# First modulation weights loaded ahead, squares summed on TensorE, modulation rows turned one piece later, filter sums by channel

## The chip, the cores and the metric

The kernel runs on one core of a Trainium2 chip. The metric is the device time of one execution in microseconds (us). Work is done by TensorE (PE), VectorE (DVE), ScalarE (ACT) and GpSimd (POOL); SyncE (SP) issues most DMAs. Each engine runs its own instructions in order, and engines wait for each other on semaphores.

## What is computed

Two layers of a generator block over 256 latent and 256 context tokens, width 1024. Cut to what the change touches:

```python
mod = silu(c) @ w_ada[li] + b_ada[li]                 # and the same of c_ctx; 6 pieces of 1024: sh1, sc1, g1, ...
h   = x * rsqrt(mean(x*x) + EPS) * norm1 * (1 + sc1) + sh1
p   = h @ w_in                                        # then four mixers, merge, MLP
# Hyena filters, of both layers and two orders n:
hdn  = sin(freq1 * (sin(freq0 * (feats @ w1 + b1)) @ w2 + b2))
taps = stack of (hdn @ w3) * decay                    # 512 channels
taps = taps / sum(abs(taps), axis=positions)          # one sum for each channel
K    = rfft(taps)
```

## The kernel before

Activations stand as features by tokens: `xT` is 8 pieces k of 128 features by 512 tokens. Weights stream from HBM in strips of 512 KB through the four slots of `raw`. The products of the layers are made of 128x512 matmuls in which both sides are split in a high and a low part (three matmuls for one, line L660, helper `mm3`); other products are plain float32 (L655, helper `mm`), and the trace counts two MATMULs for each of these.

The change lies in the start (`start_` of each engine, ahead of `dn(0)`) and in `dn(0)`, the first product, where filters of the second layer are interleaved by chunk (`between`). In the start PE does, in an order written out by hand: `columns` (turns the small vectors), `filter_angles`, eight pieces `mod_group(0, g)` of the modulation (each two strips of `w_ada`; 8 matmuls of 256 columns, weights 32 columns wide), each followed by `mod_turn(0, g - 1)` of the row before, which ACT has copied in `mod_row`; the turns of x (L766); `filter_taps`, `filter_scale` (the sum of |taps| over all positions, by 4 matmuls with the matrix of ones, after which DVE's `reciprocal` has 128x512 elements), `filter_spectrum` (16 MATMULs in the trace for one order) and `filter_nyquist` (4). The loads of strips wait for the slots of `raw`, which the pieces before must have read; x is loaded after the fourth strip. POOL squares x and adds the squares up (L3397, L3399). When the last piece of the modulation is turned, DVE makes `amp`, POOL multiplies the odd pieces of x with it (L3405) and with `rstd` (L3432), DVE the even ones (L2750), ACT adds the shift and rounds to the high part `hhl`, DVE makes the low part (L2739), and PE's `feature_strips("dn", 0)` follows piece by piece.

Four `work_bank`s of PSUM are filled in order (`fill`); a fill waits until the bank's last reader has given it back.

## Time and profile before

| | us |
|---|---|
| median of 3 runs | 1946.11 (1945.92 to 1949.07) |
| profiled execution, first to last instruction | 1946.3 |
| PE busy | 1873.7 (96%) |
| DVE busy | 1284.9 (66%) |
| ACT busy | 788.5 (41%) |
| POOL busy | 608.5 (31%) |
| 16 DMA engines, mean | 130 GB/s |

A busy PE is one with a matmul in its pipeline; it isn't PE at its full rate. The profile also tells the TensorE clock that was granted, as a share of 2.4 GHz. Before its first record it prints 1.00, whatever the clock was; the durations tell more there.

### The profile page before, as it was taken

What the parts mean: (1) busy time and instruction counts of PE and PEld (TensorE: products, weight loads), DVE (VectorE), ACT (ScalarE), POOL (GpSimd) and SP (SyncE); (2) the same over time, 40 slices, a digit from 0 to 9 for tenths busy, and PEclk for the clock granted to TensorE, in tenths of its full rate; (3) what the DMA queues carried; (4) which work ended last, traced back from release to release, by engine and by line L of the source; (5) the groups of instructions that cost most, each with busy time, mean ns of one, the idle gap of its engine ahead of it and who ended that gap; (6) DMA issues with size and microseconds to landing.
All of it is one profiled execution on the core that took longest, in us unless ns stands there. A gap on an engine that the chain in (4) does not pass through costs nothing.

```text
span 1946.3 us, 32006 instructions
## 1 busy us (share of the span) xinstructions
PE 1873.7 (96%) x11146; PEld 1525.9 (78%) x11146; DVE 1284.9 (66%) x2122; ACT 788.5 (41%) x1627; POOL 608.5 (31%) x553
## 2 busy tenths in 40 slices
PE   6999899999999999999999999999998899999999
PEld 2556788767588888877888887787787789999999
DVE  4754867666856755358765776759686655567574
ACT  2325633356243333333222232356535545445453
POOL 3433243722312111163200223444555521143030
PEclk8999899999999999999999999999999999999999
DMA  6433111232234443344555556233214335554554
GB/s 226 139 107 105 38 56 55 87 121 80 84 130 152 130 161 118 95 134 160 185 173 186 174 194 196 87 87 87 77 44 136 104 109 176 177 168 156 180 183 140
DMA packets 210925, 252.98 MB, mean 130 GB/s; under 512 B 11715, under 2 KB 176900, under 8 KB 209796
## 3 DMA queue, kind: packets, MB, share of 16 engines
q1 hardware_dynamic: 207088, 235.01, 38.2%
q10 hardware_dynamic: 3732, 16.60, 2.3%
q8 instruction: 61, 1.00, 0.2%
q14 instruction: 44, 0.36, 0.1%
HBM read 245.29 MB, written 6.29 MB: 129 GB/s over the span
## 4 chain that ended last, share of the span: by engine, by line
PE 73%; issue 10%; DVE 8%; POOL 5%; ACT 4%; DMA 1%; ACTq 1%; DVEq 0%; POOLq 0%
PE psum L660 58%; PE psum L655 13%; POOL whl L1544 2%; DVE big L2570 2%; PE psum L766 1%; POOL big L3537 1%; ACT whl L1535 1%; ACT big L1783 1%; ACT big L1786 1%; PE psum L628 1%; DVE hhl L2739 1%; DVE big L2579 1%; POOL big L1634 1%; DMA big<-in_hy_table_dram 1%; DVE big L2722 1%
## 5 line engine op out<-in xcount | busy, mean ns | idle before, releaser
L660 PE MATMUL psum<-hhl,whl 128*128 128x512 f32 (+1 forms) x4416 | 826.6, 346 | 11.6 <-DVE hhl L2739 4.3
L660 PEld LDWEIGHTS psum<-hhl,whl 128*128 128x128 f32 x4416 | 693.3, 190 | 132.4 <-issue 24.8
L1535 ACT CAST whl<-raw 128x512 fp32r<-128x512 f32 x656 | 374.1, 618 | 811.6 <-PE psum L660 806.6
L1544 DVE TENSOR_TENSOR whl<-raw,whl 128x512 fp32r<-128x512 f32 x480 | 333.6, 736 | 315.3 <-ACT whl L1535 314.4
L660 PE MATMUL psum<-bigr,whl 128*128 128x512 f32 (+1 forms) x2688 | 474.9, 337 | 1.5 <-DVEq L3314 0.7
L660 PEld LDWEIGHTS psum<-bigr,whl 128*128 128x128 f32 x2688 | 412.8, 190 | 57.2 <-issue 2.2
L1544 POOL TENSOR_TENSOR whl<-raw,whl 128x512 fp32r<-128x512 f32 x176 | 233.6, 1349 | 377.5 <-ACT whl L1535 359.0
L655 PE MATMUL psum<-big 128*128 128x128 f32 (+8 forms) x1572 | 245.7, 326 | 17.9 <-DMA big<-in_hy_w_dram 5.4
L655 PEld LDWEIGHTS psum<-big 128*128 128x128 f32 (+4 forms) x1572 | 164.5, 175 | 77.3 <-issue 51.8
L3537 POOL TENSOR_TENSOR big<-big,tmp 128x512 f32<-128x512 f32 (+1 forms) x64 | 64.5, 1021 | 341.3 <-DVE tmp L3311 340.7
L660 PE MATMUL psum<-whl,hhl 128*128 128x512 f32 x672 | 160.1, 396 | 11.0 <-POOL whl L1544 9.1
L660 PEld LDWEIGHTS psum<-whl,hhl 128*128 128x128 f32 x672 | 125.6, 190 | 40.1 <-POOL whl L1544 12.2
L1786 ACT COPY big<-psum 128x512 f32<-128x512 f32 (+3 forms) x182 | 90.3, 497 | 131.3 <-PE psum L655 93.3
L1596 POOL TENSOR_TENSOR tmp<-tmp 128x512 f32<-128x512 f32 (+1 forms) x32 | 31.3, 979 | 320.1 <-ACT tmp L1783 320.1
L2722 DVE SCALAR_TENSOR_TENSOR big<-big,csil 128x512 f32<-128x512 f32 x112 | 87.9, 785 | 5.2
L1783 ACT ACTIVATE big<-psum 128x512 f32<-128x512 f32 (+3 forms) x142 | 65.9, 475 | 26.3 <-PE psum L655 10.8
L3405 POOL TENSOR_SCALAR big<-xT,amp 128x256 f32<-128x256 f32 x48 | 54.3, 1143 | 37.9 <-issue 26.7
L2703 DVE SCALAR_TENSOR_TENSOR big<-big,csil 128x512 f32<-128x512 f32 x84 | 64.4, 819 | 1.8 <-DVE tmp L3311 1.8
L2570 DVE TENSOR_TENSOR big<-psum,big 128x512 f32<-128x512 f32 (+2 forms) x74 | 47.5, 642 | 22.1 <-PE psum L655 19.1
L2574 DVE TENSOR_SCALAR big<-psum,cols 128x512 f32<-128x512 f32 (+1 forms) x48 | 31.8, 662 | 45.1 <-PE psum L660 27.0
L2579 DVE SCALAR_TENSOR_TENSOR big<-psum,cols,big 128x510 f32<-128x510 f32 (+1 forms) x96 | 58.4, 608 | 2.6
L1783 ACT ACTIVATE big<-psum,small 128x512 f32<-128x512 f32 (+2 forms) x72 | 40.8, 594 | 39.8 <-DVE small L2576 21.7
(187 smaller groups left out, 1524.9 us busy)
## 6 DMA issues: line engine op xcount, KB each, us to landing
raw<-in_w_mlp_dram SPq DMA_DIRECT2D x128, 512.0 KB, 3.8
raw<-in_w_in_dram SPq DMA_DIRECT2D x88, 512.0 KB, 3.7
big<-in_w_ada_dram SPq DMA_DIRECT2D x88, 512.0 KB, 5.1
raw<-in_w_gate_dram SPq DMA_DIRECT2D x64, 512.0 KB, 3.5
raw<-in_w_branch_dram SPq DMA_DIRECT2D x32, 512.0 KB, 3.5
raw<-in_w_ada_dram SPq DMA_DIRECT2D x24, 512.0 KB, 5.3
raw<-in_w_o_dram SPq DMA_DIRECT2D x16, 512.0 KB, 3.5
hy_spectra<-big ACTq DMA_DIRECT2D x2, 2560.0 KB, 9.3
```

What stands on the lines that cost most here:

```text
L655: return nc.tensor.matmul(o_, a, b, start=start, stop=stop)
L660: m = nc.tensor.matmul(o_, a(p_), b(q_), start=first and i == 0, stop=last and i == 2, skip_group_check=shared)
L1535: nc.scalar.copy(whl[:, r, 0, ks], raw_of(n)[:, ks]).then_inc(S["hi_ready"], 1)
L1544: ins = eng.tensor_tensor(whl[:, r, 1, ks], raw_of(n)[:, ks], whl[:, r, 0, ks].bitcast(F32), ALU.subtract)
L1783: return nc.scalar.activation(o_, i_, fn, **kw)
L1786: return nc.scalar.copy(o_, i_)
L2570: step(V.tensor_tensor(o_, a, b, op), s_)
L2579: step(V.scalar_tensor_tensor(o_, a, sc, b, op0, op1), s_)
L2703: V.scalar_tensor_tensor(um_acc[:, r, :] if k == 7 else um_part[:, r, :], um_raw[k // 2][:, k % 2, :], csil[:, k, r:r + 1], um_part[:, r, ...
L2722: ins = V.scalar_tensor_tensor(vm_acc if k == 7 else vm_part, w, c_, vm_part, MUL, ADD)
L3405: ins = G.tensor_scalar(hn[:, k, sl], xT[:, k, sl], amp[:, li, which, k, s_:s_ + 1], None, ALU.mult)
L3537: G.tensor_tensor(m_acc[:, i, tk], m_acc[:, i, tk], tmp[:, i % 2, tk], ALU.add)\
```

## The change

All eight first pieces of `w_ada` get buffers of their own (`mod_raw`, in memory that is free until the first norm), and their loads are issued ahead, after x, without a wait; `mod_group` becomes `first_mod` for them. The small rows are issued by ACT instead of SP, the filter tables by SP instead of ACT. Two strips of the first product are loaded after the sum of squares is done. ACT squares x (into `raw`), PE sums the 8 squares with the matrix of ones (8 plain matmuls instead of 2), POOL no longer does so. `rstd` is so there long before `amp`, and POOL multiplies all 8 pieces of x with it (`first_norm`); then, after `amp`, DVE and POOL multiply and add in one operation, and ACT only copies.

Each row of the modulation is turned one piece of work later than it is made. `filter_scale` sums by channel: 16 matmuls, with |taps| as 128x128 weights and one column of ones, give 4 columns; DVE's `reciprocal` has 128x4 elements, and a new `filter_inverse` spreads the result (4 matmuls of 128 columns on PE, a copy on DVE). `filter_nyquist(0, 1)` moves from `dn(0)` into the start; `filter_sums(0, 1)` moves from DVE to POOL; `keep_spectra(0)` is issued after `gates()`.

```diff
...
+        mod_raw = [v.rearrange("p (k c) -> p k c", k=KD) for v in
+                   (arena[:, 8192:12288], whl_plain[:, :], hhl_plain[:, 0:4096], hhl_plain[:, 4096:6144],
+                    hhl_plain[:, 6144:8192])]
+        x_sq = raw[:].rearrange("p r k c -> p (r k c)").rearrange("p (k t) -> p k t", k=KD)
+        FCOL = 640
...
+        def mod_part(g):
+            return (g // 2, g % 2 * STRIP) if g < 6 else (g - 3, 0)
...
+            def first_mod(g):
+                bank = unit()
+                at, c0 = mod_part(g)
+                pe.wait_ge(mod_loaded[at], 16)
+                for k in range(KD):
+                    m = mm(bank[32 * (k % 4):32 * (k % 4) + 32, 0:STRIP], csil[:, k, :],
+                           mod_raw[at][:, k, c0:c0 + STRIP], k < 4, k >= 4)
+                m.then_inc(unit_done, 1)
...
                 pe.wait_ge(S["hyf_taps"], 2 * li + n + 1)
                 b = fill(("fs", li, n))
-                for i in range(4):
-                    m = mm(b, ones, f_z1[li][n][:, i, :], i == 0, i == 3)
+                for c_ in range(4):
+                    for i in range(4):
+                        m = mm(b[:, c_:c_ + 1], f_z1[li][n][:, i, c_ * P:(c_ + 1) * P], ones[:, 0:1],
+                               i == 0, i == 3)
                 m.then_inc(filled, 1)
-            def filter_spectrum(li, n):
+            def filter_inverse(li, n):
+                pe.wait_ge(S["hyf_cols"], 2 * li + n + 1)
+                b = fill(("fi", li, n))
+                for c_ in range(4):
+                    c0 = FCOL + 8 * li + 4 * n + c_
+                    m = mm(b[:, c_ * P:(c_ + 1) * P], small[:, c0:c0 + 1].to_broadcast([P, P]), ident)
+                m.then_inc(filled, 1)
+            def filter_spectrum(li, n, fcs=range(4)):
...
             def start_():
                 pe.wait_ge(consts_loaded, 16)
+                filter_angles(0)
+                pe.wait_ge(x_loaded, 32)
+                for k in range(KD):
+                    b = fill(("x", k))
+                    turn(b, [stage[:, m, k * P:(k + 1) * P] for m in range(NT)]).then_inc(filled, 1)
                 columns(0)
-                filter_angles(0)
+                columns(1)
                 pe.wait_ge(S["cT_ready"], 2)
-                for g in range(FIRST_MODS):
-                    mod_group(0, g)
-                    if g == 0:
-                        filter_angles(1)
-                    if g == 1:
-                        pe.wait_ge(x_loaded, 32)
-                        for k in range(KD):
-                            b = fill(("x", k))
-                            turn(b, [stage[:, m, k * P:(k + 1) * P] for m in range(NT)]).then_inc(filled, 1)
-                        filter_taps(0, 0)
-                    if g == 2:
-                        filter_taps(0, 1)
-                        columns(1)
-                    if g == 4:
-                        filter_scale(0, 0)
-                    if g == 6:
-                        filter_spectrum(0, 0)
-                        filter_nyquist(0, 0)
-                mod_turn(0, FIRST_MODS - 1)
+                first_mod(0)
+                filter_angles(1)
+                b = fill(("ms", 0, 0))
+                def squares_summed(ks):
+                    for k in ks:
+                        pe.wait_ge(S["x_ready"], KD + k + 1)
+                        m = mm(b, ones, x_sq[:, k, :], k == 0, k == KD - 1)
+                    return m
+                squares_summed(range(4))
+                mod_turn(0, 0)
+                first_mod(1)
+                squares_summed(range(4, KD)).then_inc(filled, 1)
+                mod_turn(0, 1)
+                filter_taps(0, 0)
+                first_mod(2)
+                filter_taps(0, 1)
+                mod_turn(0, 2)
+                filter_scale(0, 0)
+                first_mod(3)
+                filter_inverse(0, 0)
+                filter_spectrum(0, 0, (0, 1))
+                mod_turn(0, 3)
+                first_mod(4)
+                filter_spectrum(0, 0, (2, 3))
+                mod_turn(0, 4)
                 filter_scale(0, 1)
+                first_mod(5)
+                filter_nyquist(0, 0)
+                mod_turn(0, 5)
+                first_mod(6)
+                filter_inverse(0, 1)
+                filter_spectrum(0, 1, (0,))
+                mod_turn(0, 6)
+                first_mod(7)
+                filter_spectrum(0, 1, (1,))
+                mod_turn(0, 7)
+                filter_spectrum(0, 1, (2, 3))
+                filter_nyquist(0, 1)
...
                             gates()
-                        if chunk == 4:
-                            filter_nyquist(0, 1)
                         if chunk in (4, 12):
                             filter_taps(1, chunk // 12)
                         if chunk in (8, 16):
                             filter_scale(1, chunk // 16)
+                        if chunk in (9, 17):
+                            filter_inverse(1, chunk // 17)
...
-            load_rows(0)
             sp.dma_start(tab[:], table).then_inc(consts_loaded, 16)
-            for n in range(first_strip["dn", 0]):
-                load_strip(n)
-                if n == 2:
-                    load_rows(1)
-                if n == 3:
-                    sp.dma_start(stage[:, 0:2, :], ctx[0].rearrange("(m p) d -> p m d", p=P)).then_inc(x_loaded, 16)
-                    sp.dma_start(stage[:, 2:4, :], x[0].rearrange("(m p) d -> p m d", p=P)).then_inc(x_loaded, 16)
-                if n == 7:
-                    load_vecs(0)
+            sp.dma_start(stage[:, 0:2, :], ctx[0].rearrange("(m p) d -> p m d", p=P)).then_inc(x_loaded, 16)
+            sp.dma_start(stage[:, 2:4, :], x[0].rearrange("(m p) d -> p m d", p=P)).then_inc(x_loaded, 16)
+            def load_first_mods(g):
+                at, _ = mod_part(g)
+                src = w_ada[0][:, STRIP * g:STRIP * g + mod_raw[at].shape[2]]
+                sp.dma_start(mod_raw[at], src.rearrange("(k p) n -> p k n", p=P)).then_inc(mod_loaded[at], 16)
+            def load_filter_table(dst, src):
+                sp.dma_start(dst, src).then_inc(hyt_loaded, 16)
+            load_first_mods(0)
+            load_filter_table(f_w3.rearrange("p a b -> p (a b)"), hy_w3.rearrange("l a b -> (l a) b"))
+            load_filter_table(f_decay.rearrange("p a b c -> p (a b c)"), decay)
+            load_first_mods(2)
+            load_filter_table(f_dft.rearrange("p a b -> p (a b)"), hy_table[:, 0:1024])
+            load_first_mods(4)
+            sp.wait_ge(filled, fill_at["ms", 0, 0] + 1)
+            for n in range(2):
+                load_strip(first_strip["dn", 0] + n)
+            load_first_mods(6)
+            load_first_mods(7)
             for li in range(DEPTH):
-                for n in range(first_strip["dn", li], first_strip["merge", li]):
-                    if li and n == first_strip["dn", li] + RAW:
+                for n in range(first_strip["dn", li] + (0 if li else 2), first_strip["merge", li]):
...
             def start_():
                 load_filter()
+                load_rows(0, act)
+                load_rows(1, act)
+                def x_copy(k):
+                    b = filled_bank(act, ("x", k))
+                    step(copy(xT[:, k, :], b), S["x_ready"])
+                    give_fill(act, ("x", k))
+                def x_square(k):
+                    step(f(x_sq[:, k, :], xT[:, k, :], ACT.Square), S["x_ready"])
+                for k in range(4):
+                    x_copy(k)
+                filter_sine(0)
+                for k in range(4, KD):
+                    x_copy(k)
                 act.wait_ge(S["cols_ready"], 1)
                 for s_ in range(2):
                     step(f(csil[:, :, s_], cols[:, 0, 1, 36 + 8 * s_:44 + 8 * s_], ACT.Silu), S["cT_ready"])
-                filter_sine(0)
-                for g in range(FIRST_MODS):
+                for k in range(4):
+                    x_square(k)
+                mod_row(0, 0)
+                for k in range(4, KD):
+                    x_square(k)
+                filter_sine(1)
+                mod_row(0, 1)
+                log_exp_tables()
+                b = filled_bank(act, ("ms", 0, 0))
+                rsqrt(rstd[:], b, D, S["rstd_ready"], after=lambda: give_fill(act, ("ms", 0, 0)))
+                for g in range(2, 7):
                     mod_row(0, g)
-                    if g == 0:
-                        load_filter_tables()
-                        filter_sine(1)
-                        log_exp_tables()
-                    if g in (2, 3):
-                        filter_taps(0, g - 2)
-                    if g == 1:
-                        for k in range(KD):
-                            b = filled_bank(act, ("x", k))
-                            step(copy(xT[:, k, :], b), S["x_ready"])
-                            give_fill(act, ("x", k))
+                    if g in (2, 4):
+                        filter_taps(0, g // 4)
                 for i in range(RING):
                     split_hi(act, split_strips[i])
+                mod_row(0, 7)
+                for k in range(KD):
...
+                    copy(hhl[:, 0, k, :], HN[0][:, k, :]).then_inc(S["hhi_ready"], 1)
...
             def filter_scale(li, n):
                 b = filled_bank(dve, ("fs", li, n))
-                step(V.reciprocal(f_inv[n], b))
+                c0 = FCOL + 8 * li + 4 * n
+                step(V.reciprocal(small[:, c0:c0 + 4], b[:, 0:4]), S["hyf_cols"])
                 give_fill(dve, ("fs", li, n))
-            def filter_spectrum(li, n):
+            def filter_inverse(li, n):
+                b = filled_bank(dve, ("fi", li, n))
+                cp(f_inv[n], b)
+                give_fill(dve, ("fi", li, n))
...
                 filter_angle(0)
+                columns(0)
+                columns(1)
                 filter_angle(1)
-                for g in range(FIRST_MODS):
-                    mod_cols(0, g)
-                    if g == 0:
-                        filter_cut(0, 0)
-                        filter_sums(0, 0)
-                    if g == 1:
-                        filter_cut(0, 1)
-                        columns(1)
-                    if g == 2:
-                        filter_sums(0, 1)
-                    if g == 3:
-                        filter_scale(0, 0)
-                    if g == 5:
-                        filter_spectrum(0, 0)
-                        filter_nyquist(0, 0)
-                amps(0, 0)
+                mod_cols(0, 0)
+                mod_cols(0, 1)
+                filter_cut(0, 0)
+                filter_sums(0, 0)
+                filter_cut(0, 1)
+                mod_cols(0, 2)
+                filter_scale(0, 0)
+                filter_inverse(0, 0)
+                filter_spectrum(0, 0, (0, 1))
+                mod_cols(0, 3)
+                filter_spectrum(0, 0, (2, 3))
+                mod_cols(0, 4)
+                filter_scale(0, 1)
+                filter_nyquist(0, 0)
+                mod_cols(0, 5)
                 for i in range(RING):
                     split_lo(dve, split_strips[i])
-                filter_scale(0, 1)
+                filter_inverse(0, 1)
+                filter_spectrum(0, 1, (0,))
+                mod_cols(0, 6)
+                filter_spectrum(0, 1, (1,))
+                mod_cols(0, 7)
+                amps(0, 0)
+                first_norm()
+            def first_norm():
+                hn = HN[0]
+                def scaled(k):
+                    dve.wait_ge(S["xa_ready"], k + 1)
+                    for s_ in range(2):
+                        sl = slice(s_ * L, (s_ + 1) * L)
+                        ins = V.tensor_scalar(hn[:, k, sl], hn[:, k, sl], amp[:, 0, 0, k, s_:s_ + 1],
+                                              mod[:, 0, k, s_:s_ + 1], MUL, ADD)
+                    ins.then_inc(S["hn_dve"], 1)
+                def low(k):
+                    nm, count = hn_ready(0, k)
+                    dve.wait_ge(S[nm], count)
+                    dve.wait_ge(S["hhi_ready"], k + 1)
+                    signals(dve, V.tensor_tensor(hhl[:, 1, k, :], hn[:, k, :], hhl[:, 0, k, :].bitcast(F32), SUB),
+                            S["h_ready"])
+                scaled(0)
+                scaled(2)
+                low(0)
+                low(1)
...
+                low(7)
+                dve.wait_ge(S["h_ready"], KD)
+                filter_spectrum(0, 1, (2, 3))
+                filter_nyquist(0, 1)
+                layer_vecs(0)
...
+            def first_norm():
+                hn = HN[0]
+                pool.wait_ge(S["rstd_ready"], 1)
+                for k in range(KD):
+                    G.tensor_tensor(hn[:, k, :], xT[:, k, :], rstd[:], ALU.mult).then_inc(S["xa_ready"], 1)
+                pool.wait_ge(S["xa_ready"], KD)
+                filter_sums(0, 1)
+                pool.wait_ge(S["amp_ready"], 1)
+                for k in range(1, KD, 2):
...
+                    ins.then_inc(S["hn_pool"], 1)
+                pool.wait_ge(S["h_ready"], KD)
...
```

## Rows read from the trace of the kernel before

**Rows 1.** The page, section 1: busy time, share of the span, instructions.
```profile
PE 1873.7 (96%) x11146; PEld 1525.9 (78%) x11146; DVE 1284.9 (66%) x2122; ACT 788.5 (41%) x1627; POOL 608.5 (31%) x553
```

**Rows 2.** The chain of waits, start: start us, us, what.
```profile
6.37 6.53 DMA big<-in_hy_w_dram
```

**Rows 3.** PE's timeline, 12 to 30 us: start us, us, group, idle before.
```profile
12.94 1.22 PE L655 MATMUL psum<-big 33*128 33x256 f32 x2 [5.36 <-DMA big<-in_hy_w_dram]
...
19.35 1.94 PE L655 MATMUL psum<-raw,csil 128*32 128x256 f32 x16
...
29.57 6.39 PE L655 MATMUL psum<-big 64*128 64x512 f32 x8 [1.08 <-DMA big<-in_hy_table_dram]
```

**Rows 4.** PE's timeline, 38 to 100 us.
```profile
38.38 7.19 PE L655 MATMUL psum<-big 64*128 64x512 f32 x8
...
54.43 1.07 PE L655 MATMUL psum<-raw,csil 128*32 128x256 f32 x16
55.43 0.44 PE L760 MATMUL psum<-tab,rows 128*128 128x128 f32 x2
...
57.08 8.75 PE L655 MATMUL psum<-big 128*128 128x512 f32 x20
...
79.62 1.95 PE L660 MATMUL psum<-hhl,whl 128*128 128x512 f32 x6
82.85 1.65 PE L660 MATMUL psum<-hhl,whl 128*128 128x512 f32 x6 [1.27 <-DVE hhl L2739]
85.46 11.20 PE L660 MATMUL psum<-hhl,whl 128*128 128x512 f32 x48 [0.96 <-DVE hhl L2739]
96.49 5.77 PE L655 MATMUL psum<-big 128*128 128x512 f32 x12
```

**Rows 5.** Busy time in stretches; the last three numbers: PEclk, DMA share, GB/s.
```profile
30.40:50.80 20.40, 20.40 (x71) 7.23 (x70) 14.27 (x21) 3.06 (x7) 11.46 (x9) 0.50 0.37 104
81.50:85.00 3.50, 1.73 (x7) 1.05 (x6) 3.50 (x5) 1.25 (x4) 2.43 (x2) 1.00 0.00 0
...
197.60:201.00 3.40, 2.29 (x21) 2.18 (x21) 2.93 (x7) 0.61 (x3) 3.40 (x2) 1.00 0.36 102
...
248.80:252.20 3.40, 3.40 (x9) 2.65 (x9) 3.12 (x9) 0.89 (x2) 0.57 (x1) 0.50 0.50 134
```

**Rows 6.** ACT's timeline, 8 to 55 us.
```profile
8.39 0.47 ACT L1783 ACTIVATE csil<-cols 128x8 f32<-128x8 f32 x2
...
25.06 5.47 ACT L1786 COPY xT<-psum 128x512 f32<-128x512 f32 x8
...
52.19 2.19 ACT L1783 ACTIVATE big<-big 128x512 f32<-128x512 f32 x4 [3.03 <-DVE big L2570]
```

**Rows 7.** DVE's timeline, 36 to 53 us.
```profile
36.00 0.69 DVE L2570 TENSOR_TENSOR big<-psum,big 128x512 f32<-128x512 f32 x1 [1.02 <-PE psum L655]
36.84 6.21 DVE L2570 TENSOR_TENSOR big<-big 128x512 f32<-128x512 f32 x4
...
49.23 2.87 DVE L2570 TENSOR_TENSOR big<-big 128x512 f32<-128x512 f32 x4
```

**Rows 8.** POOL's timeline, 30 to 80 us.
```profile
40.92 1.59 POOL L3399 TENSOR_TENSOR tmp<-tmp 128x512 f32<-128x512 f32 x1
...
78.58 5.35 POOL L3432 TENSOR_TENSOR big<-big,rstd 128x512 f32<-128x512 f32 x4
```

**Rows 9.** PE's timeline, 184 to 320 us: small matmuls with 128x128 weights.
```profile
184.27 0.75 PE L655 MATMUL psum<-small,tab 128*128 128x16 f32 x6
184.86 3.03 PE L660 MATMUL psum<-hhl,whl 128*128 128x512 f32 x12
...
195.47 4.08 PE L655 MATMUL psum<-tri_r,g_hl 128*128 128x128 f32 x32
200.66 1.72 PE L655 MATMUL psum<-big 128*128 128x128 f32 x8 [1.11 <-DVEq L1513]
...
283.50 31.96 PE L655 MATMUL psum<-big 128*128 128x128 f32 x272
```

More of the change, by code:

```diff
@@ L158, in sbr @@
             return es.enter_context(nc.sbuf_tensor(name, shape, F32R))
+        with nc.sbuf_tensor("whl_plain", [P, RING * 2 * KS * STRIP], F32) as whl_plain:
+            pass
         whl = sbr("whl", [P, RING, 2, KS, STRIP])
+        with nc.sbuf_tensor("hhl_plain", [P, 2 * KD * T], F32) as hhl_plain:
+            pass
         hhl = sbr("hhl", [P, 2, KD, T])
@@ L392, in build @@
         vm_loaded = [sem(f"vm_loaded{i}") for i in range(4)]
+        mod_loaded = [sem(f"mod_loaded{i}") for i in range(len(mod_raw))]
         unit_done = sem("unit_done")
@@ L551, in add_mods @@
                     group_of[len(strips) - 1] = li, g
-        add_mods(0, range(FIRST_MODS))
         for li in range(DEPTH):
@@ L2541, in _ @@
             for li in range(DEPTH):
[L2542 removed]
+                if li:
+                    norm(li, 0)
                 dn(li)
@@ L2642, in start_ @@
                 step(V.memset(csil[:], 0.0))
-                columns(0)
                 for r in range(2):
@@ L2744, in scaled @@
                 def scaled(k):
-                    if nn:
-                        dve.wait_ge(S["xa_ready"], KD * (nn - 1) + k + 1)
-                        ins = V.tensor_tensor(hn[:, k, tk], hn[:, k, tk], rstd[:, tk], MUL)
-                    for s_ in ss if nn == 0 else ():
-                        sl = slice(s_ * L, (s_ + 1) * L)
-                        ins = V.scalar_tensor_tensor(hn[:, k, sl], xT[:, k, sl],
-                                                     amp[:, li, which, k, s_:s_ + 1], rstd[:, sl], MUL, MUL)
-                    ins.then_inc(S["hn_dve"], 1)
-                scaled(0)
-                if nn:
-                    scaled(1)
-                    low(0)
-                    scaled(2)
-                    low(1)
-                else:
-                    scaled(2)
-                    low(0, 1)
+                    dve.wait_ge(S["xa_ready"], KD * nn + k + 1)
+                    V.tensor_tensor(hn[:, k, tk], hn[:, k, tk], rstd[:, tk], MUL).then_inc(S["hn_dve"], 1)
+                scaled(0)
+                scaled(1)
+                low(0)
+                scaled(2)
+                low(1)
                 scaled(4)
@@ L3006, in dn @@
                     conv_block(1)
-                    filter_nyquist(0, 1)
                     filter_cut(1, 0)
@@ L3013, in dn @@
                     dve.wait_ge(spectra_kept, 16)
+                    filter_inverse(1, 0)
                     filter_spectrum(1, 0)
@@ L3023, in dn @@
                     conv_block(8)
+                    filter_inverse(1, 1)
                     filter_spectrum(1, 1)
@@ L3425, in norm @@
-                pool.wait_ge(S["rstd_ready"], n + 1)
-                if n:
-                    nm, count = hn_ready(n, 1)
-                    pool.wait_ge(S[nm], count)
-                if n:
-                    pool.wait_ge(S["h_ready"], KD * n + 1)
-                for k in range(3 if n else 1, KD, 2):
+                pool.wait_ge(S["amp_ready"], n + 1)
+                for k in range(KD):
+                    pool.wait_ge(S["x_added"], 24 * li + 8 * which - 7 + k)
+                    if k < KD - 2:
+                        squared(k)
+                    scaled(k, S["xa_ready"])
```

150 lines of the change are left out of this document (71 added, 79 removed).

## The prediction

> **What bounds the kernel now.** I read the page first: PE is busy for 96% of the span [rows 1], so what a change is worth is PE time, and time in which PE waits or runs at half clock. Then the chain of waits, for the start: it runs over small transfers issued by ACT until 12.90 us, when the first filter matmul can go [rows 2]. Then PE's timeline: from 29.57 to 81.6 us PE has hardly a gap [rows 3, 4], and from 85.46 on it streams the first product. So the start, too, is bound by PE and not by the loads of the weights. But the stretches show the granted clock at 0.50, the 1.2 GHz level, from 30.4 to 50.8 us [rows 5]; a piece of the modulation takes 1.94 us at half clock and 1.07 at the full 2.4 GHz [rows 3, 4]. Half of 20.4 us, some 10.2 us, is what that clock costs before.
>
> **The point to beat.** The first 60 split matmuls (6, 6 and 48) are done at 96.5 us, with waits of 1.27 and 0.96 us between them [rows 4]. At 11.20 / 48 = 0.233 us each they take 14.0 us: before is as good as a kernel that starts this product at 82.5 us and never waits. The 4 MATMULs of `filter_nyquist(0, 1)` then come inside the product; at 8.75 / 20 = 0.44 us each [rows 4] they are 1.75 us, and in the changed kernel they come ahead of it. So the changed kernel gains at the start if its `dn(0)` begins before 84.2 us and then doesn't wait. The end of the sum is 1946.3 us, the profiled span; the median of the runs is 0.2 us below.
>
> **Part 1, to the first piece.** The first filter matmul still waits for ACT's small loads: 12.9 us, done 14.2 [rows 2, 3]. Behind it in PE's order now stand the turns of x. They are paced by ACT's copies, 5.47 / 8 = 0.68 us each [rows 6], with a sine in their middle (an estimate of 0.4 us, by the 0.55 us of 512 columns in rows 6): from 15.0 to 21.0. The small vectors are turned meanwhile, their 12 loads now behind the filter's on ACT's queue; two Silus, 0.47 us together [rows 6], and hand-overs give 21.9 us for `first_mod(0)`. A table load of ScalarE before the Silu, or small loads that lag behind the larger packets of SP, would add 1 to 4 us; a gain isn't to be seen here. I take none.
>
> **Part 2, to the sum of squares.** At half clock: a piece 1.93, the second filter matmul 1.22 (as the first, rows 3), one 512-column matmul 7.19 / 4 = 1.8 [rows 4]; together 4.9, to 26.8. By then PE has streamed 128x128x512 work without a gap, and I let the clock rise. Then seven squares at 0.88 (6.1), a turn 0.44 and a piece 1.07 [rows 4]: 34.4. All at full clock would be 32, all at half 42. ACT's squares (8 of some 0.6) stay ahead. This sum is 8 matmuls on PE where 2 were, 5.3 us more PE work; POOL's chain of squares, which it replaces, wasn't late.
>
> **Part 3, a wait that isn't there before.** PE goes on with a turn, `filter_taps(0, 0)`, a piece, `filter_taps(0, 1)`, a turn: 0.44 + 3.5 + 1.07 + 3.5 + 0.44 = 8.95, to 43.4. `filter_scale(0, 0)` stands next and needs |taps| from ACT, which needs `filter_sums(0, 0)` from DVE. DVE has the last cut product at 34.4 + 0.44 + 3.5 + 0.7 = 39.0 (0.69 each, rows 7). Its four sums took 6.21 us while POOL was at its own two-input operations, and 2.87 when POOL was idle [rows 7, 8]. In the changed kernel POOL has just been given `rstd` (34.4 + 1.6 us) and multiplies 8 pieces at 5.35 / 4 = 1.34 us or slower: it is busy from 36.0 to over 46.7, over the whole of the sums. So 39.0 + 6.2 = 45.2, ACT's four absolute values 2.19 [rows 6] and hand-overs: 47.7. PE waits 4.3 us; with sums of 2.87 it would be 1.0. Behind the waiting instruction stands all the rest of PE's start; in the kernel before two pieces of the modulation lie between, and 2 us of slack.
>
> **Part 4, the sums by channel.** 16 plain matmuls are 32 MATMULs with 128x128 weights each. Matmuls of 16 and 32 columns followed each other at (184.86 - 184.27) / 6 = 0.098 us, such of 128 columns at 31.96 / 272 = 0.1175 [rows 9]: these are times of the weight load, not of the columns. So 3.1 to 3.8 us, I take 3.6: nothing gained against the 8 MATMULs of 0.44 = 3.5 before. At half clock it is 8 in 1.72, 0.215 each [rows 9], 6.9 us. `filter_inverse` is 8 more MATMULs, 0.9 us. DVE is spared 4 x 3.4 us of reciprocals less 4 copies, but DVE holds nobody up there. The Trainium skill, "TensorE: Matmul & The Clock Gate", Part 1, gives a floor of about 25 ns from start to start for matmuls of few columns; by it a sum would be 32 x 0.025 = 0.8 us, 2.8 us less at each of four places. The row with its own weights for each matmul speaks against it.
>
> What such a sum does to the clock is the disputed price. It was at full after 81.50:85.00, in which PE was busy for 1.73 of 3.50 us with 512-column matmuls; it fell to half at 201 after 197.60:201.00, in which PE was counted busy for 2.29 of 3.40 us, but with 128-column matmuls at 0.12 us, which leave the columns idle for half of that time, and a gap of 1.11 [rows 5, 9]. So what counts isn't that PE is "busy" with weight loads but that columns pass. In a sum by channel one column passes per 0.11 us, for 3.6 us. I take it that the clock falls at each of the four. A fall costs 3.4 us at half clock, as in 248.80:252.20 [rows 5], that is 1.7 us of PE time, plus what is left of the sum itself: 2.0 us. The bounds are 0 and 5 us each.
>
> **Part 5, the sum of the start.** The rest after 47.7 at full clock: two sums 7.2, five pieces 5.35, two `filter_inverse` 1.8, the spectra 32 x 0.44 = 14.0, two nyquists 3.5, five turns 2.2; 34.0, to 81.7. After the wait of 4.3 us the clock is at half; the first sum by channel can't raise it (3.3 more), nor what follows until a full half spectrum has run (1.7 more), and the second sum costs 1.7: 6.7, to 88.4. Against 84.2 that is 4.2 us slower. The end of the start is covered: when the last row is turned, 6 MATMULs of the last spectrum and nyquist blocks x 2 (12 x 0.44 = 5.3 us) run while DVE makes `amp` and the first pieces, some 3 us; then a piece is needed each 1.4 us and POOL delivers two in 2.3. The waits of 1.27 and 0.96 us go; nothing is late next.
>
> **Part 6, in `dn(0)`.** PE has no gap there, so all counts: two `filter_inverse` 1.8 us, two sums by channel that cost what they did, and two falls of the clock at 2.0: 5.8 us. The moved `keep_spectra` transfer must land before chunk 10's filter; about 9 us of copy behind `gates()` against some 14 us: free. All else follows at the same pace. The loads themselves, ahead by tens of us, remove no wait that the chain shows; what they allow is the earlier order.
>
> **Sum:** 1946.3 + 4.2 + 5.8 = 1956.3, at the median 1956.
>
> **Rivals.** (a) Weight loads hold the clock up: for it, PE is counted busy in them, and at 283.50 (rows 9) 32 us of matmuls with only half of the time in columns kept it. Then the sums lower nothing: the start ends near 83.5 (the wait of 4.3 and one half-clock stretch stay), the product costs 1.8: 1946.3 - 0.7 + 1.8 = 1947.4. (b) The other side, faster: DVE and POOL don't meet, or the absolute values come in time, so that PE hardly waits at `filter_scale(0, 0)`, and the clock stays up from about 27 us. It is decided by whether the sums of DVE end before about 42.5 us. Then 43.4 + 1.0 + 34.0 = 78.4, less 5.8 at the start, plus 1.8: 1942.3; with the clock up from 21.9 on, 1940. For it: the half-clock stretch of 20.4 us is what before pays most for, and dense squares could end it for good. (c) The small loads on ACT's queue come 3 to 4 us later behind larger packets, and all shifts: 1960. (d) Few-column matmuls run at the floor that the skill tells of: 1956.3 - 11.2 = 1945, and less where the clock then holds.
>
> **Chances.** Forecast 0.50 (1951 to 1960), (a) 0.20, (b) 0.15, (c) 0.10, (d) 0.05. The range has to reach (b)'s upper part and (c): 1942 to 1961. A measurement of this kernel can tell about 0.2%, 3.9 us. Faster than 1942.2: 0.15, from (b); within: 0.28, from (a), (d) and the lower edge of the forecast; slower: 0.57.
>
> **What would show it.** Right: a gap of PE of about 4 us before the first sum by channel, released by ACT; DVE's four sums taking about 6 us beside POOL; granted clock 0.50 after each sum by channel, also twice between 100 and 180 us; 32 MATMULs of one column in 3.1 to 3.8 us; the first L660 group near 88 us. Wrong: clock 1.00 through those sums, or the first L660 before 82 us. The point at which I am least sure is the clock.

## The result, and the profile after

The changed kernel is slower: 1963.72 us (median of 4 runs, 1962.21 to 1965.16) against 1947.59 (4 runs, 1945.92 to 1949.4) of the kernel before, ratio 1.0083 [1.0069, 1.0097]. The spans of the profiled executions, from first to last instruction, differ by 13.8 us (1960.1 against 1946.3). The direction was forecast; the time lies 2.7 us above the range's upper end. An execution takes longer than its span: 2.4 to 2.7 us in the four of the changed kernel (the profiled one 1962.69 and 1960.1), to which the section on the prediction comes back.

PE has 10 us more busy time than in rows 1. The page, section 1:

```profile
PE 1883.6 (96%) x11286; PEld 1545.0 (79%) x11286; DVE 1271.9 (65%) x2114; ACT 793.5 (40%) x1628; POOL 601.5 (31%) x548
```

PE's timeline of the start (start us, us, group, idle before):

```profile
14.39 1.19 PE L668 MATMUL psum<-big 33*128 33x256 f32 x2 [14.39 <-DMA big<-in_hy_w_dram]
...
26.24 1.94 PE L668 MATMUL psum<-big,csil 128*32 128x256 f32 x16 [2.66 <-ACT csil L1846]
...
29.12 4.38 PE L668 MATMUL psum<-raw,tab 128*128 128x512 f32 x8
...
34.66 3.70 PE L668 MATMUL psum<-raw,tab 128*128 128x512 f32 x8
...
51.53 6.99 PE L668 MATMUL psum<-tab,big 128*128 128x1 f32 x32 [4.32 <-ACT big L1846]
58.45 1.93 PE L668 MATMUL psum<-whl_plain,csil 128*32 128x256 f32 x16
60.31 1.67 PE L668 MATMUL psum<-tab,small 128*128 128x128 f32 x8
...
70.33 3.63 PE L668 MATMUL psum<-tab,big 128*128 128x1 f32 x32
...
90.53 14.21 PE L673 MATMUL psum<-hhl,whl 128*128 128x512 f32 x60
```

Groups like those of rows 3 and 4 come in another order now. The one-column groups are the sums by channel; the first runs at half clock, after the wait of 4.32 us, and takes 6.99 us. The `128x128 x8` group is `filter_inverse`. The first split matmul (L673 is L660 of before) starts at 90.53 us. Matched one to one, the first split matmul behind these 60 starts 6.1 us later than before (108.3 and 102.2 us; in both kernels it stands behind the moved `filter_nyquist(0, 1)`), the one at 236.0 us (222.1 before), after the last filter of the second layer, 13.9 us later, and the last one of all 13.8. So the loss is made in the start and in `dn(0)`, and nothing is lost or regained behind.

DVE's four sums and POOL's products behind that wait, and ACT's table loads ahead of the first piece:

```profile
43.08 6.11 DVE L2645 TENSOR_TENSOR big<-big 128x512 f32<-128x512 f32 x4
```

```profile
39.91 11.64 POOL L3541 TENSOR_TENSOR big<-xT,rstd 128x512 f32<-128x512 f32 x8 [39.48 <-ACT rstd L1846]
```

```profile
13.04 1.28 ACT L1849 ACT_TABLE_LOAD   x1 [13.04 <-issue]
...
19.91 1.28 ACT L1846 ACT_TABLE_LOAD   x1
...
24.43 1.28 ACT L1846 ACT_TABLE_LOAD   x1
25.73 0.46 ACT L1846 ACTIVATE csil<-cols 128x8 f32<-128x8 f32 x2
```

The stretches at half clock and a pair of groups in `dn(0)`. In the first fence the columns are the stretch, its length, busy time (and instructions) of PE, PEld, DVE, ACT and POOL, then PEclk, DMA share and GB/s:

```profile
23.90:30.70 6.80, 4.46 (x20) 2.10 (x21) 1.36 (x5) 6.40 (x12) 0.00 (x0) 0.50 1.04 391
51.20:61.40 10.20, 9.87 (x53) 8.59 (x54) 2.81 (x5) 0.65 (x2) 5.40 (x5) 0.50 0.23 47
75.10:78.50 3.40, 3.40 (x5) 1.24 (x5) 0.00 (x0) 0.34 (x1) 0.00 (x0) 0.50 0.00 0
129.70:133.10 3.40, 3.40 (x10) 2.63 (x9) 0.00 (x0) 0.00 (x0) 0.00 (x0) 0.50 0.67 289
170.60:177.40 6.80, 6.80 (x23) 5.82 (x23) 1.47 (x7) 3.70 (x14) 0.00 (x0) 0.50 0.00 1
```

```profile
125.75 3.73 PE L668 MATMUL psum<-tab,big 128*128 128x1 f32 x32 [0.64 <-ACT big L1846]
129.34 4.60 PE L673 MATMUL psum<-hhl,whl 128*128 128x512 f32 x12
...
167.70 4.33 PE L668 MATMUL psum<-tab,big 128*128 128x1 f32 x32
...
172.64 5.24 PE L673 MATMUL psum<-hhl,whl 128*128 128x512 f32 x12
```

The second stretch begins 0.3 us ahead of the first sum by channel, at the end of PE's wait, and the last three in or just behind a sum; the kernel before has none between 50.8 and 201 us. Twelve split matmuls take 3.03 us in rows 9; behind the sums they take 4.60 and 5.24.

### The profile page after: what moved, and what is told of

Its sections match the earlier page's. It is cut to its first block, busy times and chain, and to the rows that moved or that the text cites. A ratio compares the mean times of both kernels' runs of the same rounds, so it can differ in the third digit from the quotient of the medians.

```text
span 1960.1 us, 32265 instructions
## 1 busy us (share of the span) xinstructions
PE 1883.6 (96%) x11286; PEld 1545.0 (79%) x11286; DVE 1271.9 (65%) x2114; ACT 793.5 (40%) x1628; POOL 601.5 (31%) x548
## 4 chain that ended last, share of the span: by engine, by line
PE 74%; issue 8%; DVE 7%; POOL 4%; ACT 3%; ACTq 0%; DVEq 0%; POOLq 0%
PE psum L673 58%; PE psum L668 13%; POOL whl L1596 2%; DVE big L2645 2%; PE psum L787 1%; POOL big L3655 1%; ACT whl L1587 1%; PE psum L641 1%; ACT big L1846 1%; ACT big L1849 1%; DVE big L2984 1%; DVE big L2654 1%; DVE hhl L2861 1%; POOL big L1686 1%; DVE big L2844 1%
## 5 line engine op out<-in xcount | busy, mean ns | idle before, releaser
L673 PE MATMUL psum<-hhl,whl 128*128 128x512 f32 (+1 forms) x4416 | 828.0, 346 | 7.9 <-DVE whl L1596 3.7
L673 PEld LDWEIGHTS psum<-hhl,whl 128*128 128x128 f32 x4416 | 694.2, 190 | 129.2 <-issue 23.6
L673 PE MATMUL psum<-bigr,whl 128*128 128x512 f32 (+1 forms) x2688 | 474.9, 337 | 1.6 <-DVEq L3427 0.7
L673 PEld LDWEIGHTS psum<-bigr,whl 128*128 128x128 f32 x2688 | 412.7, 190 | 57.3 <-issue 2.2
L668 PE MATMUL psum<-big 128*128 128x128 f32 (+8 forms) x1572 | 241.2, 323 | 25.5 <-DMA big<-in_hy_w_dram 14.4
L673 PE MATMUL psum<-whl,hhl 128*128 128x512 f32 x672 | 161.9, 399 | 10.6 <-POOL whl L1596 8.6
L673 PEld LDWEIGHTS psum<-whl,hhl 128*128 128x128 f32 x672 | 126.8, 191 | 40.4 <-POOL whl L1596 11.9
L787 PE MATMUL psum<-tab,big 128*128 128x128 f32 x296 | 47.4, 306 | 9.0 <-DVEq L1565 5.0
```

Of the source, the lines that this page charges most:

```text
L668: return nc.tensor.matmul(o_, a, b, start=start, stop=stop)
L673: m = nc.tensor.matmul(o_, a(p_), b(q_), start=first and i == 0, stop=last and i == 2, skip_group_check=shared)
L787: m = nc.tensor.transpose(bank[:, i * P:(i + 1) * P], s, ids)
```

## The experiments

Theory C: the sums by channel cost time through the clock. Rival W: what costs is waiting (POOL beside DVE, late small loads, table loads). In the table "start" is the shift of the first split matmul behind the first 60, and "`dn(0)`" the further shift up to the one that starts at 222.1 us before, both in us and in one profile of each kernel against that of before.

| kernel | median us | ratio to before | start | `dn(0)` |
|---|---|---|---|---|
| changed | 1963.72 | 1.0083 [1.0069, 1.0097] | +6.1 | +7.8 |
| sums by ones | 1949.12 | 1.0016 [1.0006, 1.0025] | +0.4 | +0.8 |
| sums of 128 columns | 1953.4 | 1.0040 [1.0026, 1.0054] | +1.4 | +1.9 |
| POOL after the sums | 1957.22 | 1.0059 [1.0041, 1.0076] | +3.2 | +6.6 |
| one table | 1960.23 | 1.0058 [1.0039, 1.0076] | +3.9 | +7.6 |
| before, with channel sums | 1970.36 | 1.0128 [1.0110, 1.0147] | +11.2 | +8.8 |
| three undone | 1942.63 | 0.9972 [0.9961, 0.9984] | -8.1 | +1.1 |
| the same again | 1943.29 | 0.9982 [0.9972, 0.9993] | -4.0 | +0.7 |

**The changed kernel with the old sum by the matrix of ones** (no `filter_inverse`).

```diff
-                for c_ in range(4):
-                    for i in range(4):
-                        m = mm(b[:, c_:c_ + 1], f_z1[li][n][:, i, c_ * P:(c_ + 1) * P], ones[:, 0:1],
-                               i == 0, i == 3)
+                for i in range(4):
+                    m = mm(b, ones, f_z1[li][n][:, i, :], i == 0, i == 3)
...
```

> The changed kernel with one part undone: the sums of |taps| again by 4 matmuls of 512 columns with the matrix of ones, the reciprocal of 128x512, and no spreading of the result. Theory C (a sum by channel passes one column per 0.11 us, and the clock falls behind it): 3.6 us of spreading go, in the first product 10 us at half clock (5 us), in the start a sum of 3.5 instead of 7.0 us and about 1.5 us more: 13 to 14 us less, 0.993 of the changed kernel, 1950 us. In the trace the clock stays at 1.00 between 110 and 200 us. Rival W (weight loads keep PE active, and the falls in the changed kernel come from its waits and the phase): only the spreading goes, 3.6 us, 1960 us, and the half-clock stretches at some 130 and 170 us stay.

Measured 1949.12 us. PE's timeline, and the stretches where the changed kernel was at half clock in `dn(0)`:

```profile
51.02 6.72 PE L668 MATMUL psum<-big,tab 128*128 128x512 f32 x8 [4.33 <-ACT big L1840]
...
67.28 3.60 PE L668 MATMUL psum<-big,tab 128*128 128x512 f32 x8
...
84.87 14.18 PE L673 MATMUL psum<-hhl,whl 128*128 128x512 f32 x60
```

```profile
129.70:133.10 3.40, 3.40 (x9) 1.52 (x8) 2.91 (x5) 0.00 (x0) 0.12 (x1) 1.00 0.55 154
170.60:177.40 6.80, 6.80 (x18) 2.97 (x17) 3.85 (x6) 0.00 (x0) 0.00 (x0) 1.00 0.25 76
```

The wait is the same, 4.33 us, and 14.6 of the 16.1 us are gone by the medians, 12.9 of the 13.8 by the profiles. This is as C said: from the start of the first sum to the product it is 33.85 us where the changed kernel needs 39.0, and the clock stays at 1.00 in the two stretches of `dn(0)`. But the first sum takes 6.72 us here too, where the second takes 3.60: the clock falls at 50.3 us, in the wait, for 6.8 us. So the first fall isn't made by the sum by channel, which only prolongs it, to 10.2 us.

**The changed kernel with sums by channel of 128 equal columns**: the same 32 MATMULs with the same weights, but columns pass.

```diff
-                        m = mm(b[:, c_:c_ + 1], f_z1[li][n][:, i, c_ * P:(c_ + 1) * P], ones[:, 0:1],
+                        m = mm(b[:, c_ * P:(c_ + 1) * P], f_z1[li][n][:, i, c_ * P:(c_ + 1) * P], ones,
...
```

> The changed kernel with the same 16 weight loads for each sum by channel, but 128 columns of ones in place of one (the reciprocal takes each 128th column). Theory C: the matmuls still follow each other at 0.11 us, but columns pass for half of the time, as in the stretch at 283.5 us of the kernel before, where the clock held: no fall behind the sums of the first product, 5 us less, and 1 to 3 us in the start: 1956 to 1958 us. Rival W: nothing changes, 1963 to 1964 us, half-clock stretches as before.

Measured 1953.4, more gained than C had said. PE's timeline, and a stretch behind the wait:

```profile
51.47 5.32 PE L668 MATMUL psum<-tab,big 128*128 128x128 f32 x32 [4.34 <-ACT big L1846]
...
67.22 3.74 PE L668 MATMUL psum<-tab,big 128*128 128x128 f32 x32
```

```profile
54.60:61.40 6.80, 6.80 (x51) 4.66 (x50) 1.57 (x3) 0.37 (x1) 3.50 (x3) 1.00 0.00 0
```

At full clock 128 columns cost what one does (3.74 and 3.63 us), so the weight loads set the pace; and the clock comes up during the first sum and holds through the other three. The weight loads are the same in both kernels and the columns are not: it is the passing columns that hold the clock here. Of the 14.6 us, 10.3 are this; the other 4.3 lie between this kernel and the one with sums by ones, which has no `filter_inverse`.

**The changed kernel with POOL's products held back until DVE's sums are done.**

```diff
                 pool.wait_ge(S["rstd_ready"], 1)
+                pool.wait_ge(S["hyf_sums"], 1)
```

> The changed kernel, but POOL starts its 8 multiplications by rstd only when DVE has made the first filter's sums. Theory P (DVE and POOL slow each other): DVE's four sums take 2.9 us instead of 6.1, PE's wait before the first sum by channel falls from 4.3 to about 1.0 us, and the clock may still be full in it: 3 to 6 us less, 1958 to 1961 us. Rival: the sums are slow by themselves, and the wait stays at 4 us: 1964 us. POOL's work has 30 us of idle time behind it, so its delay should cost nothing.

Measured 1957.22. DVE's timeline, then PE's:

```profile
43.34 2.87 DVE L2645 TENSOR_TENSOR big<-big 128x512 f32<-128x512 f32 x4
```

```profile
48.54 6.90 PE L668 MATMUL psum<-tab,big 128*128 128x1 f32 x32 [1.08 <-ACT big L1846]
```

The four sums take 2.87 us instead of 6.11 and PE's wait is 1.08 instead of 4.32: that is POOL's part, 3.2 us. The sum still takes 6.90 us, at half clock: the fall doesn't need the long wait. The spans differ by 5.8 us: 2.9 in the start, 1.1 in `dn(0)`, where the second fall lasts 3.4 us and not 6.8, and 1.8 behind it, where nothing was changed. Only the first is shown to be POOL's; the others may be scatter.

**The changed kernel with one table set for the start**, one that holds both functions, loaded ahead of the copies.

```diff
+                nc.scalar.preload_act_table_set("silu_and_others")
                 def x_copy(k):
```

> The changed kernel with the table of Silu and sine loaded once, ahead of ACT's copies. In the changed kernel ACT loads tables at 13.0, 19.9 and 24.4 us, each 1.28 us, where the kernel before loads once; PE then waits 2.66 us for the Silus. Theory T: two loads go from the path, the first piece of the modulation begins 2.6 us earlier and all behind it: 1961 us, 0.9987 of the changed kernel. Rival: something else holds the Silus (the small vectors), and the time stays within 1 us.

Measured 1960.23. ACT's timeline, then PE's:

```profile
12.24 1.28 ACT L1890 ACT_TABLE_LOAD   x1 [12.24 <-issue]
...
22.65 0.46 ACT L1846 ACTIVATE csil<-cols 128x8 f32<-128x8 f32 x2
```

```profile
23.16 1.07 PE L668 MATMUL psum<-big,csil 128*32 128x256 f32 x16 [1.39 <-ACT csil L1846]
```

Without two of its three table loads, the first piece starts 3.1 us earlier than in the changed kernel (26.24), and here at full clock. It takes 1.80 to 1.94 us in all four profiles with three loads and 1.07 in four of the six with one. The first sum by channel starts 4.9 us earlier, but the product only 2.2: PE waits 4.65 us ahead of that sum, and the half-clock stretches at the first two sums are 13.6 and 6.8 us long where they were 10.2 and 3.4.

**The kernel before with the sums by channel alone** (and `filter_inverse` ahead of each spectrum).

> The kernel before with this one part alone: sums by channel and the spreading, both layers, all else as before. Theory C: spreading 3.6 us, in the first product two falls (5 us or less by phase), in the start one or two falls (2 to 5 us): 10 to 14 us more than before, 1957 to 1961 us. Rival W: 3.6 us more, 1951 us. DVE's 4 reciprocals of 3.4 us go either way and should bring nothing.

Measured 1970.36, more than either theory had said. The first product costs 8.8 us (7.8 in the changed kernel), but PE has a new wait:

```profile
89.98 3.78 PE L656 MATMUL psum<-big 128*128 128x512 f32 x4 [9.87 <-DVEq L1528]
```

A `filter_inverse` and the 4 fills of one spectrum are 5 fills on 4 banks, and PE waits until DVE has given the bank back by its copy at 89.17 us, which stands behind its work for the norm. The start of this kernel is therefore no price of the sums; it shows why the changed kernel places the spectrum in parts.

**Three parts undone**: the changed kernel with the first, third and fourth of these edits together.

> The changed kernel with the old sums, POOL behind DVE's sums, and one table. If the terms add (old sums 14.6 us less, POOL 6.5, of which some 3 are the clock and may be gone with the old sums, table 2.6): 1942 to 1946 us, 0.998 to 1.000 of the kernel before, the first split matmul at about 79 us. Rival: the terms overlap, because PE or the loads of the weights become the bound, and it stays at 1948 us as with the old sums alone.

Measured 1942.63, and 1943.29 in the second timing below: 0.2 to 0.3% faster than the kernel before. In the profiles the three edits gave 12.9, 5.8 and 2.7 us by themselves, 21.4 together, and 20.7 as one.

**Then the parts that are left: squares on POOL again** (as before; the last square on ACT, two matmuls on PE), the rest as in three undone.

```diff
-                squares_summed(range(4))
                 mod_turn(0, 0)
                 first_mod(1)
-                squares_summed(range(4, KD)).then_inc(filled, 1)
...
+                pe.wait_ge(S["sq_seventh"], 1)
+                mm(b, ones, x_sq[:, KD - 1, :], True, False)
+                pe.wait_ge(S["sq_first"], 1)
+                mm(b, ones, tmp[:, 1, :], False, True).then_inc(filled, 1)
```

> As the kernel with three parts undone (old sums, POOL behind DVE, one table), and the squares of x again squared and added on POOL (the last one on ACT), summed by 2 matmuls behind the first taps. Expectation: 5.3 us of PE work go from a start that PE bounds: 3 to 5 us less than the kernel with three parts undone, 1938 to 1942 us. Rival: PE needs the dense squares to bring the clock up at 30 us; without them the taps run at half clock as in the kernel before, and the gain is lost (within 1 us of that kernel or slower).

Measured 1951.83 (1.0022 [1.0011, 1.0034]), 9 us above three undone. DVE's timeline in this kernel, DVE's in three undone, then PE's and a stretch of this kernel:

```profile
17.05 3.86 DVE L2642 SCALAR_TENSOR_TENSOR big<-big 128x256 f32<-128x256 f32 x3
...
29.57 3.58 DVE L2637 TENSOR_SCALAR big<-big 128x256 f32<-128x256 f32 x3
```

```profile
25.72 0.95 DVE L2645 TENSOR_SCALAR big<-big 128x256 f32<-128x256 f32 x3
26.70 1.35 DVE L2650 SCALAR_TENSOR_TENSOR big<-big 128x256 f32<-128x256 f32 x3
```

```profile
35.83 0.69 PE L781 MATMUL psum<-tab,rows 128*128 128x128 f32 x2 [5.03 <-ACT rows L1839]
```

```profile
33.80:47.50 13.70, 11.67 (x29) 4.42 (x30) 7.20 (x15) 2.44 (x4) 0.00 (x0) 0.50 0.02 6
```

POOL's chain slows DVE's arguments of the sine, one operation almost threefold and the other almost fourfold; ACT waits for them in its order ahead of a row's copy, PE waits 5.03 us, and 13.7 us at half clock follow. The first split matmul starts at 87.03 us, and at 76.30 and 80.41 in the two profiles of three undone. So the squares on TensorE, which cost PE 5.3 us, are worth 9 in this order.

**The kernel before with three matmuls of 512 columns behind the turns of x**, to keep the clock from falling at 30.4 us.

```diff
+                        cover(("start", 0), 3)
                         filter_taps(0, 0)
```

> The kernel before with three matmuls of 512 columns that nobody reads between the turns of x and the first filter taps, where PE waits 1.1 us for a table. Theory C: the clock then doesn't fall at 30 us, so that the 20 us at half clock go; PE catches up with DVE's contended sums and waits for those instead (3 to 4 us at about 40 us), and the cover costs 1.6 us: 1940 to 1943 us. Rival: the half-clock stretch comes from the narrow taps (64 rows) and pieces themselves, the clock falls anyway, and it is 1947 to 1948 us.

Measured 1947.12 (1.0004 [0.9994, 1.0015]). The stretches, then PE's timeline:

```profile
30.40:44.10 13.70, 9.96 (x38) 3.72 (x36) 10.28 (x11) 2.78 (x6) 12.10 (x10) 1.00 0.40 111
44.10:50.90 6.80, 6.63 (x40) 3.00 (x41) 5.36 (x11) 0.64 (x2) 0.00 (x0) 0.50 0.51 160
```

```profile
44.27 0.40 PE L815 MATMUL psum<-tab,rstd 100*128 100x100 f32 x1 [3.91 <-DVEq L1514]
```

The clock stays up for 13.7 of the 20.4 us that rows 5 show at half, which is worth 6.8 us of PE time, and PE spends them: the cover takes 2.8 us, and PE waits 3.91 us for DVE, which is at its four sums, 5.84 us beside POOL, much as in rows 7. The first split matmul starts 0.6 us earlier, and the median is the same. In the prediction I had priced half of 20.4 us as "what that clock costs before"; for the 13.7 us that this run removes, it cost about nothing.

**Rows turned at once** in three undone: `mod_turn(0, g)` right behind `first_mod(g)`, for rows 2 to 7.

> The kernel with three parts undone, with each modulation row from the third on (rows 2 to 7, six of them) turned right behind its own piece and not one piece of other work later. Theory T (the delay hides ACT's copy of the row): PE waits some 0.65 us before each of the six turns (a hand-over, a copy of 0.37 us, a hand-over), 3.9 us in all, seen as waits released by ACT at the turns; median 1946 to 1947. Rival N (PE's other queueing or the wait before the first filter sum absorbs it): no waits at the turns over 0.2 us, median within 1 us of the kernel with three parts undone.

Measured 1942.39 (0.9988 [0.9978, 0.9998]), against 1943.29 (0.9982) of the kernel it is built on, in the same set. PE's timeline shows the waits of theory T (five of 0.54 us and one of 0.49, 3.2 in all), but a shorter wait at the first filter sum, and the clock at 1.00 there:

```profile
38.52 0.44 PE L781 MATMUL psum<-tab,rows 128*128 128x128 f32 x2 [0.54 <-ACT rows L1843]
...
43.07 3.70 PE L668 MATMUL psum<-big,tab 128*128 128x512 f32 x8 [0.48 <-ACT big L1840]
```

The first split matmul starts at 77.80 us, between the 76.30 and 80.41 of the two profiles of three undone. So a gain from the later turns, 1.5 us by the faster of these, isn't to be told from the scatter or in the medians: T was right on the waits and wrong on the time.

**A cover ahead of the first filter sum** in three undone.

> The kernel with three parts undone, with three 512-column matmuls whose result nobody reads (1.3 us) put ahead of the first filter sum, where PE waits 1.08 us for ACT and the granted clock is 0.50 for the stretch behind it. Theory G (the fall comes from the gap): the wait is below 0.3 us, the clock stays at 1.00 there, and the sum and its followers end some 1.5 us earlier: 1 to 2 us below the kernel with three parts undone in the profile. Rival F (the fall has another cause, or the time comes back as a wait later): the clock still falls between 41 and 48 us, or the first split matmul starts no earlier than 76 us.

Measured 1942.45 (0.9980 [0.9971, 0.9990]). PE's timeline:

```profile
41.92 2.74 PE L641 MATMUL psum<-tab 128*128 128x512 f32 x6
44.50 3.60 PE L668 MATMUL psum<-big,tab 128*128 128x512 f32 x8
```

No wait, and full clock; but three matmuls are 6 MATMULs and 2.74 us, not the 1.3 I had counted, and the product starts at 76.26 where it did at 76.30. The cover cost what it saved, which is rival F's second sign; the clock did as G said.

**Three parts undone, again.**

> The kernel with three parts undone once more, beside the two that are built on it. If the first timing holds, the median is 1941 to 1944 and the interval of the ratio lies below 1; if it was a lucky set, it comes out within 2 us of the kernel before.

Measured 1943.29: it holds. Its profiled execution is 6.0 us longer than the first one (1945.4 and 1939.4) of the same instructions. PE's timelines, first profile and second:

```profile
23.29 1.07 PE L668 MATMUL psum<-big,csil 128*32 128x256 f32 x16 [1.38 <-ACT csil L1840]
...
43.20 5.27 PE L668 MATMUL psum<-big,tab 128*128 128x512 f32 x8 [1.08 <-ACT big L1840]
...
76.30 14.21 PE L673 MATMUL psum<-hhl,whl 128*128 128x512 f32 x60
```

```profile
24.11 1.93 PE L668 MATMUL psum<-big,csil 128*32 128x256 f32 x16 [1.38 <-ACT csil L1840]
...
45.64 3.70 PE L668 MATMUL psum<-big,tab 128*128 128x512 f32 x8 [1.08 <-ACT big L1840]
...
61.03 5.40 PE L668 MATMUL psum<-big,tab 128*128 128x512 f32 x8 [1.99 <-ACT big L1840]
...
80.41 11.95 PE L673 MATMUL psum<-hhl,whl 128*128 128x512 f32 x50
```

The same wait of 1.08 us is followed by half clock once and by full clock once. Where the clock changes differs from one execution to the next, and the start differs by 4.1 us with it.

## Why the prediction was right or wrong

**The mechanism was right.** Forecast and measured: the wait ahead of the first sum by channel 4.3 and 4.32 us, from the sums of DVE beside POOL (6.2 and 6.11); 32 MATMULs of one column 3.6 and 3.63 us at full clock, 6.9 and 6.99 at half; two falls of the clock in `dn(0)`. The leg from the first piece to the sum of squares was 12.5 and 12.1 us. The Trainium skill, "GPSIMD Engine Reference", section 1, says that GpSimd shares its SBUF interfaces with VectorE and that they contend at operations with two SBUF inputs; the traces agree, 6.11 us beside POOL and 2.87 alone. Rival (d), by which one-column matmuls would follow each other at the floor of about 25 ns that the Trainium skill gives in "TensorE: Matmul & The Clock Gate", Part 1, fell: they went at 3.63 / 32 = 0.113 us, with own weights for each matmul. That is above the floor and doesn't contradict it; a lower bound was no price for them.

**The first step that failed is Part 1's "I take none".** The first piece was forecast at 21.9 us and started at 26.24, 4.3 us later. I had named a table load of ScalarE and late small loads, 1 to 4 us, and put nothing of it in the sum. Two table loads stand behind the first four copies and ahead of the Silus, 1.28 us each; with one table the piece comes 3.1 us earlier. The first filter matmul is 1.45 us later than in rows 3; that the queues' changed order does this is not shown by a run of its own. Together these are 4.0 of the 4.3 us. The Trainium skill, "ScalarE: Activation LUTs", section "Table sets: the hidden batching unit", says to group the functions by table set; moving the sine between copies and Silu did the opposite, and the trace shows the two loads of 1.28 us for it. The delay was carried on: the sum of channels began at 51.53 and not at 47.7 us.

**The second is the size of Part 6.** `dn(0)` lost 7.8 us and not 5.8. Counted from start to start, against the same groups of before: the two `filter_inverse` cost 0.8 and 0.9 us, 1.7, as forecast. The first sum and its fall cost 0.4 of waiting, 0.45 in the sum and 1.4 in the split matmuls behind it, 2.3. The second cost 0.65 in the sum, 0.4 in a group of turns and 2.2 in the split matmuls, 3.3. Another 0.5 is added behind them, up to 236 us, where both kernels have stretches at half clock. The term that was too small is the 2.0 us for a fall: the second lasted 6.8 us at half clock, where I had taken the shortest stretch of rows 5 for both.

**Part 5 was 1.7 us too dear**: from the first sum to the product 39.0 us, not 40.7. That hid a part of the first error, by luck. So the product starts 4.3 - 0.4 - 0.1 - 1.7 = 2.1 us later than forecast, and 1.9 us of that are left in the 6.1 us of the start (4.2 forecast); with the 2.0 us in `dn(0)`, 10.0 became 13.8 us, profile to profile, and 1956.3 became 1960.1.

**The third step that failed is the base of the sum.** I set the span beside the median, found 0.2 us between them and forecast 1956 for both. But the changed kernel's median is 3.6 us above its profiled span: its executions take 2.4 to 2.7 us more than their spans, and the profiled one was 1.0 us faster than its median. For the kernel before, all 65 executions whose span is on record take 1.8 to 2.0 us more, so that its profiled span of 1946.3 would belong to an execution of about 1948.2 (an estimate; that execution's own time isn't on record), 0.6 above the median of 1947.59. By this estimate the two kernels differ by 0.7 us in what an execution adds to its span, and 0.7 + 1.0 + 0.6 = 2.3 us is how 13.8 us between the profiles become 16.1 between the medians. Of the 7.7 us between the forecast of 1956 and 1963.72, 3.8 are in the spans and 3.9 are this.

The range failed by 2.7 us, less than the base step alone; the span of 1960.1 lies inside it. It was also narrow for its own terms: the named extras, 1 to 4 us of Part 1 and up to 5 us for a fall, were given chances as if only one could come; one of each at its end puts the forecast beyond 1961.

**The rivals.** (a), weight loads hold the clock up, is out: with the same loads it falls at one column and stays at 128. (b) was to be decided by whether the sums of DVE end before about 42.5 us; they ended at 49.2, beside POOL. It needed DVE and POOL apart; the kernel with three parts undone has that and the old sums, and its span, 1939.4 us, is even 2.9 below the 1942.3 of (b), which was made against the span. It was a price for another kernel. (c), late small loads, is seen with 1.45 us at the first filter matmul, not 3 to 4; most of the delay was the table loads.

How few columns would still hold the clock was not measured, and why the clock falls after a wait of 1.08 us in one execution and not in another stays open. The early loads, the first norm in one operation and the sums moved to POOL weren't undone by themselves.

## What to carry to other kernels

Sums over partitions that use the data as weights and stream one column save nothing against a 512-column matmul with the matrix of ones: they take the time of the weight loads (3.63 us where the other sum takes 3.60), and they cost clock in what follows. When steps are moved to another engine's idle time, ask first which two-input operations on DVE they will meet, and when activations are moved, which table sets they now alternate. Half clock in a stretch is a price only if nothing else would be waited for there: three matmuls that took away 13.7 us of it gained nothing. And before a span is forecast as a time, ask what an execution adds to its span, in both kernels.

## What the runs showed of the hardware that was not expected

POOL's two-input operations slowed not only DVE's sums of two tensors (2.87 to 6.11 us) but also its operations with one tensor (0.95 to 3.58 us for three of 128x256), by more. A table load was 1.28 us with 0.10 us of idle time ahead of it, so two of them are 2.6 us. And the squares of x as 8 plain matmuls, 5.3 us of work added to the busiest engine, made the kernel some 9 us faster than the same squares on POOL.
